# The inner layer norms' affine split between ScalarE and VectorE, rounded products first, and the last norm stored by half rows

## The chip, the cores and the metric

The kernel runs on one core of one Trainium2 chip. The metric is the time of one execution on the device in microseconds (us). The kernel before was timed three times: 1306.21, 1308.70 and 1308.98 us, median 1308.7. The profiled execution took 1311.17 us; its span, from the first to the last instruction of the trace, is 1309.4 us.

## What is computed

One sequence of 256 tokens of 1024 features goes through two blocks. The first has two layers (an attention and pooling mixer, then a gated linear attention mixer), each followed by an MLP; the second has a gated delta rule mixer with a spatial gating unit, and a mixture of 16 experts. Behind each mixer and each MLP stands a residual with a layer norm, six in all:

```python
def layer_norm(x, g, b):
    xf = x.astype(jnp.float32)
    mu = jnp.mean(xf, axis=-1, keepdims=True)
    var = jnp.mean(jnp.square(xf - mu), axis=-1, keepdims=True)
    return ((xf - mu) * lax.rsqrt(var + LN_EPS) * g + b).astype(x.dtype)
...
    x = layer_norm(ALPHA * x + mix, ln1_g[i], ln1_b[i])
    x = layer_norm(ALPHA * x + sqrelu_mlp(x, mlp_w1[i], mlp_w2[i]), ln2_g[i], ln2_b[i])
```

`mix` and the MLP end in a matmul over all features, and what follows a norm starts with one. So the norm stands between two stretches of TensorE work, and the weights of the first product behind it are on the chip before it begins.

## The kernel before

**Products.** Every weight matrix is streamed in chunks of 1 MB (128 partitions x 2048 numbers). SyncE loads a chunk into one of three slots of `ring`. ScalarE copies it, rounded to the matmul format, into `w_hi` (L1603); VectorE writes the rest, `ring - w_hi`, into `w_lo` (L1020). Activations are split in the same way (`x_hi`/`x_lo`, `o_hi`/`o_lo`). A product is three matmuls: hi*hi, hi*lo and lo*hi (`products`, L364 to L368). A chunk against 256 tokens is 48 matmuls of 256 columns (`by_feature`, `by_token`, `triples`), or 24 of 512 columns in the output projections (`by_rows`, `last_rows`). `take` (L358) waits until both parts of a chunk are there. `triples` is a generator that yields after every three matmuls, so that other products can be put in between.

**What sets the order.** Each engine's program is written out by hand in one block per engine. An engine works strictly in its own order and waits on semaphores: `full`/`evac` per PSUM bank, `hi_split` and `pieces_split` for weights, `normed`, `x_hi`, `x_split` for a norm. `split_ahead` puts the rounding of the next weights into the programs of ScalarE and VectorE just ahead of each read of a PSUM bank, as many chunks ahead as its argument says. SyncE issues the load of chunk n once VectorE has split chunk n-3.

**An inner norm** (five of the six, l = 0 to 4) works on two token halves t = 0, 1 of 128 tokens each, and on two feature halves.
- TensorE (`last_rows`, L450) ends the projection: token half 0 first, then the two halves of token half 1. Among the last of these it puts the eight transposes of token half 0 (`norm_transposes`, L509), then two triples of the next chunk (waiting on `x_split`), the eight transposes of token half 1, and the other 14 triples.
- VectorE (`moments`, L1040; `normalize`, L1053) adds the residual out of PSUM (L1047), takes the statistics (L1049, L1051) and writes `(x - mean) / deviation` to `res` (L1059). ScalarE takes the square root (L1625).
- The affine `* g + b` is applied to the transposed tile on its way out of PSUM into `n_v`. ScalarE does it for three of the four (token half, feature half) pairs, four tiles of 128 x 128 each (`high_half`, L1627, L1633), and rounds into `x_hi` (L1636). VectorE does the fourth (L1084, L1089). VectorE writes `x_lo` for all four (`low_half`, L1061, L1064).
- GpSimd computes the same affine for the token-major residual `xt` (`affine`, L2045: L2052 times g, L2053 plus b), while the MLP runs.

**The last norm** has no transposes: VectorE normalizes into `res`, GpSimd multiplies and adds over 1024 columns per token half, and SyncE stores each token half in one DMA (L2169).

## Time and profile before

| | |
|---|---|
| median of 3 runs | 1308.7 us |
| profiled execution, its span | 1311.17 us, 1309.4 us |
| PE (TensorE matmul) busy | 1265.4 us, 97% of the span |
| DVE (VectorE) busy | 832.6 us, 64% |
| ACT (ScalarE) busy | 600.5 us, 46% |
| POOL (GpSimd) busy | 170.2 us, 13% |
| mean granted TensorE clock | 0.987 |

Busy times of matmuls are modelled and overlap, so the share of PE says that it seldom stands still, not that it is at its peak. What a change near a norm is worth is read from the gaps between matmuls there: a timeline gives for each row its start, its duration and, in brackets, how long the engine stood idle before it and what ended that. Rows are merged where instructions of one line follow each other (x8); the start of the next row minus the start of this one is then what the group took.

### The profile page before, as it was taken

Reading aid. Unit: us, or ns where it says so; the run is one execution under the profiler, and the core shown is the slowest. Engines: PE = TensorE matmul, PEld = TensorE weight load, DVE = VectorE, ACT = ScalarE, POOL = GpSimd, SP = SyncE. Lnnn points to the kernel's source line nnn. Section 1 sums busy time; section 2 is a strip of 40 time slices with the busy share of each in tenths; the row PEclk is TensorE's granted clock in tenths of the full one; section 3 lists DMA queues with packets and bytes.
Section 4 is the critical chain, followed back from the end, with each engine's and each line's share of the span. In section 5 each row is a group of like instructions: output and inputs, shape, how many; then the busy total and the mean of one; then the engine's idle time right before and its main releaser. Section 6 shows DMA issues by size and latency. Waiting matters only on the chain.

```text
span 1309.4 us, 20713 instructions
## 1 busy us (share of the span) xinstructions
PE 1265.4 (97%) x8950; PEld 1180.4 (90%) x8950; DVE 832.6 (64%) x980; ACT 600.5 (46%) x697; POOL 170.2 (13%) x132
## 2 busy tenths in 40 slices
PE   7999999999999999999899999899999999999996
PEld 7977999998998899998889999899998999999995
DVE  6566865557655775556699448863776765555554
ACT  4464533335645533333575346624833543333331
POOL 8400400001300040000402200120000050000002
PEclk9999999999999999999989999999999999999999
DMA  9712575554643475558786447563764465555550
GB/s 269 172 65 97 165 238 182 189 192 122 201 161 97 132 255 181 181 187 142 129 143 101 97 91 126 110 107 55 225 206 162 139 204 180 187 192 191 180 176 33
DMA packets 160220, 205.02 MB, mean 157 GB/s; under 512 B 13571, under 2 KB 142322, under 8 KB 160130
## 3 DMA queue, kind: packets, MB, share of 16 engines
q1 hardware_dynamic: 157906, 195.80, 53.6%
q0 software_dynamic: 2224, 7.90, 2.0%
q8 instruction: 71, 1.16, 0.4%
q14 instruction: 19, 0.16, 0.0%
HBM read 202.63 MB, written 1.05 MB: 156 GB/s over the span
## 4 chain that ended last, share of the span: by engine, by line
PE 88%; DVE 5%; ACT 4%; DMA 2%; issue 1%; POOLq 0%; POOL 0%; DVEq 0%; ACTq 0%
PE PS L366 25%; PE PS L367 24%; PE PS L368 24%; DMA ring<-in_w_in 2%; DVE w_lo L1020 2%; PE PS L869 1%; PE PS L853 1%; PE PS L865 1%; PE PS L516 1%; ACT AR L1633 1%; ACT w_hi L1603 1%; PE PS L594 1%; PE PS L616 1%; PE PS L765 1%; PE PS L771 1%
## 5 line engine op out<-in xcount | busy, mean ns | idle before, releaser
L1020 DVE TENSOR_TENSOR w_lo<-ring,w_hi 128x2048 fp32r<-128x2048 f32 x182 | 434.7, 2392 | 207.1 <-ACT w_hi L1603 206.7
L366 PE MATMUL PS<-x_hi,w_hi 128*128 128x256 f32 x1648 | 477.2, 290 | 2.6 <-DVE w_lo L1115 2.1
L368 PE MATMUL PS<-x_hi,w_lo 128*128 128x256 f32 x1648 | 468.5, 284 | 0.0
L367 PE MATMUL PS<-x_lo,w_hi 128*128 128x256 f32 x1648 | 468.4, 284 | 0.0
L1603 ACT ACTIVATE w_hi<-ring 128x2048 fp32r<-128x2048 f32 x182 | 347.3, 1912 | 241.7 <-PE PS L368 229.2
L366 PEld LDWEIGHTS PS<-x_hi,w_hi 128*128 128x128 f32 x1648 | 318.6, 193 | 8.5 <-issue 3.4
L367 PEld LDWEIGHTS PS<-x_lo,w_hi 128*128 128x128 f32 x1648 | 318.4, 193 | 3.9 <-issue 2.2
L368 PEld LDWEIGHTS PS<-x_hi,w_lo 128*128 128x128 f32 x1648 | 318.0, 193 | 0.0
L1615 ACT ACTIVATE AR<-PS 128x512 f32<-128x512 f32 (+1 forms) x144 | 82.1, 586 | 306.5 <-PE PS L368 187.7
L366 PE MATMUL PS<-w_hi,o_hi 128*128 128x512 f32 x480 | 188.5, 393 | 1.3 <-ACT res L1615 0.8
L367 PE MATMUL PS<-w_lo,o_hi 128*128 128x512 f32 x480 | 187.4, 390 | 0.0
L368 PE MATMUL PS<-w_hi,o_lo 128*128 128x512 f32 x480 | 186.8, 389 | 0.0
L2052 POOL TENSOR_TENSOR xt<-res,gb 128x1024 f32<-128x1024 f32 x12 | 43.0, 3581 | 676.0 <-DVE res L1059 227.0
L366 PEld LDWEIGHTS PS<-w_hi,o_hi 128*128 128x128 f32 x480 | 90.3, 188 | 20.4 <-DVE o_lo L1234 1.5
L368 PEld LDWEIGHTS PS<-w_hi,o_lo 128*128 128x128 f32 x480 | 90.1, 188 | 19.2
L367 PEld LDWEIGHTS PS<-w_lo,o_hi 128*128 128x128 f32 x480 | 90.3, 188 | 16.6
L366 PE MATMUL PS<-w_hi,x_hi 128*128 128x256 f32 x256 | 77.1, 301 | 12.8 <-DVE x_lo L1064 12.0
L367 PE MATMUL PS<-w_lo,x_hi 128*128 128x256 f32 x256 | 74.3, 290 | 0.0
L368 PE MATMUL PS<-w_hi,x_lo 128*128 128x256 f32 x256 | 74.1, 289 | 0.0
L366 PEld LDWEIGHTS PS<-w_hi,x_hi 128*128 128x128 f32 x256 | 51.4, 201 | 15.2 <-issue 15.2
L1231 DVE TENSOR_TENSOR AR<-AR 128x512 f32<-128x512 f32 x32 | 23.2, 725 | 53.7 <-ACT AR L1615 53.7
L367 PEld LDWEIGHTS PS<-w_lo,x_hi 128*128 128x128 f32 x256 | 51.2, 200 | 0.2 <-issue 0.2
(370 smaller groups left out, 1341.4 us busy)
## 6 DMA issues: line engine op xcount, KB each, us to landing
ring<-in_mlp_w SPq DMA_DIRECT2D x64, 1024.0 KB, 5.3
ring<-in_w_in SPq DMA_DIRECT2D x32, 1024.0 KB, 11.5
ring<-in_expert_w_gate SPq DMA_DIRECT2D x16, 1024.0 KB, 5.4
ring<-in_expert_w_up SPq DMA_DIRECT2D x16, 1024.0 KB, 5.4
ring<-in_expert_w_down SPq DMA_DIRECT2D x16, 1024.0 KB, 4.9
ring<-in_c_w_in SPq DMA_DIRECT2D x12, 1024.0 KB, 5.5
ring<-in_a_w_in SPq DMA_DIRECT2D x4, 1024.0 KB, 8.6
ring<-in_c_w_out SPq DMA_DIRECT2D x4, 1024.0 KB, 5.0
```

The lines of the kernel that those rows point to most:

```text
L366: mm(out, a_hi, b_hi, start=first, stop=False, skip_group_check=True)
L367: mm(out, a_hi, b_lo, start=False, stop=False, skip_group_check=True)
L368: return mm(out, a_lo, b_hi, start=False, stop=last, skip_group_check=True)
L516: ins = nc.tensor.transpose(ps[:, i * P:(i + 1) * P], res[:, t, k * P:(k + 1) * P], ident[:])
L594: mm(ps[:, i * nk:(i + 1) * nk], a_q[:, head, t * P:(t + 1) * P], a_kk[:, g, a, 0:nk], start=True, stop=False, skip_group_check=True)
L616: ins = mm(PS[:, t, o:o + nh * P], a_v2[kb][:, a, 64 * g:64 * g + P], a_T[:, n % 3, kb * nh * P:(kb + 1) * nh * P], start=False, stop=(kb ...
L765: ins = mm(ps, ones[:], s_sq[:, j % 2].rearrange("p a b -> p (a b)"), start=True, stop=True)
L1020: v.tensor_tensor(w_lo[:, m % PARTS], ring[:, index[split[m]] % RING], w_hi[:, m % PARTS].bitcast(F32), ALU.subtract)\
L1231: after(v.tensor_tensor(h, h, h, ALU.mult))
L1603: a(w_hi[:, m % PARTS], ring[:, index[split[m]] % RING], ACT.Copy).then_inc(S("hi_split"), 1)
L1615: evacuated(a(out, ps if in_ is None else in_(ps), func, scale=scale), name)
L2052: after(gp.tensor_tensor(xt[:, t, :], res[:, t, :], gb[:, 0, :], ALU.mult))
```

## The change

1. **Rounded weight first.** `by_feature`, `by_token`, `triples` and `by_rows` now issue all products with `w_hi` first (32 of 48, or 16 of 24), waiting only for `hi_split`, and then those with `w_lo`, waiting for `pieces_split`. The number and shapes of matmuls stay. Not changed are the very first chunk (`halves`) and `last_rows`.
2. **Rounded x first in a norm.** The chunk behind an inner norm is taken by `with_norm`: 8 products with `x_hi` of a (token half, feature half) wait only for its `x_hi`; the 4 with `x_lo` come later. Twenty of them now stand ahead of the transposes of token half 1.
3. **Affine shared.** The four transposed tiles of a (token half, feature half) go to two banks of two tiles: ScalarE takes one bank, VectorE the other (`affine_half`). ScalarE then rounds all four into `x_hi`. VectorE loses its rounding (L1089) and gains the affine of 6 more tiles.
4. **Order on ScalarE.** In each inner norm the rounding of the next-but-one chunk moves ahead of token half 1's affine.
5. **Last norm.** VectorE does `(x - mean) * g` and `* 1/deviation + b` by halves of 512 columns with `scalar_tensor_tensor`; GpSimd is out of it. SyncE stores four half rows.

ScalarE in the first inner norm (`AR<-PS,vec` is the affine, `st<-st,cst` the square root), before:

```order
L1625 ACTIVATE st<-st,cst 128x1
L1633 ACTIVATE AR<-PS,vec 128x128 x4
L1636 ACTIVATE x_hi<-AR 128x4x128
L1633 ACTIVATE AR<-PS,vec 128x128 x4
L1636 ACTIVATE x_hi<-AR 128x4x128
L1625 ACTIVATE st<-st,cst 128x1
L1633 ACTIVATE AR<-PS,vec 128x128 x4
L1636 ACTIVATE x_hi<-AR 128x4x128
L1603 ACTIVATE w_hi<-ring 128x2048
```

and in the changed kernel:

```order
L1736 ACTIVATE st<-st,cst 128x1
L1744 ACTIVATE AR<-PS,vec 128x128 x2
L1748 ACTIVATE x_hi<-AR 128x4x128
L1744 ACTIVATE AR<-PS,vec 128x128 x2
L1748 ACTIVATE x_hi<-AR 128x4x128
L1736 ACTIVATE st<-st,cst 128x1
L1714 ACTIVATE w_hi<-ring 128x2048
L1744 ACTIVATE AR<-PS,vec 128x128 x2
L1748 ACTIVATE x_hi<-AR 128x4x128
L1744 ACTIVATE AR<-PS,vec 128x128 x2
L1748 ACTIVATE x_hi<-AR 128x4x128
```

Each affine group is halved, a fourth group is added, and the weight rounding stands ahead of token half 1.

VectorE from the reciprocal of token half 0 on, in the same norm, before:

```order
L1056 RECIPROCAL st<-st 128x1
L1059 TENSOR_SCALAR res<-res,st 128x512 x2
L1047 SCALAR_TENSOR_TENSOR res<-xt,PS 128x512
L1049 BN_STATS st<-res 128x6
L1047 SCALAR_TENSOR_TENSOR res<-xt,PS 128x512
L1049 BN_STATS st<-res 128x6
L1051 BN_AGGR st<-st 128x2
L1064 TENSOR_TENSOR x_lo<-AR,x_hi 128x4x128
L1056 RECIPROCAL st<-st 128x1
```

and in the changed kernel:

```order
L1139 RECIPROCAL st<-st 128x1
L1142 TENSOR_SCALAR res<-res,st 128x512 x2
L1128 SCALAR_TENSOR_TENSOR res<-xt,PS 128x512
L1130 BN_STATS st<-res 128x6
L1155 TENSOR_SCALAR AR<-PS,vec 128x128 x4
L1128 SCALAR_TENSOR_TENSOR res<-xt,PS 128x512
L1130 BN_STATS st<-res 128x6
L1134 BN_AGGR st<-st 128x2
L1148 TENSOR_TENSOR x_lo<-AR,x_hi 128x4x128
L1139 RECIPROCAL st<-st 128x1
```

Four affine tiles come in between the two column halves of token half 1.

VectorE at the end of the program (the last norm, from token half 1's first column half on), before:

```order
L1047 SCALAR_TENSOR_TENSOR res<-xt,PS 128x512
L1049 BN_STATS st<-res 128x6
L1047 SCALAR_TENSOR_TENSOR res<-xt,PS 128x512
L1049 BN_STATS st<-res 128x6
L1051 BN_AGGR st<-st 128x2
L1056 RECIPROCAL st<-st 128x1
L1059 TENSOR_SCALAR res<-res,st 128x512 x2
```

and in the changed kernel:

```order
L1128 SCALAR_TENSOR_TENSOR res<-xt,PS 128x512
L1130 BN_STATS st<-res 128x6
L1172 RECIPROCAL st<-st 128x1
L1175 SCALAR_TENSOR_TENSOR xt<-res,st,gb 128x512 x2
L1128 SCALAR_TENSOR_TENSOR res<-xt,PS 128x512
L1130 BN_STATS st<-res 128x6
L1134 BN_AGGR st<-st 128x2
L1168 SCALAR_TENSOR_TENSOR res<-res,st,gb 128x512 x2
L1172 RECIPROCAL st<-st 128x1
L1175 SCALAR_TENSOR_TENSOR xt<-res,st,gb 128x512 x2
```

The finish of token half 0 stands ahead of token half 1's last statistics, and what GpSimd did has come to VectorE.

The diff, cut to its core (`by_token`, `triples` and `by_rows` change as `by_feature` does):

```diff
+            def take_high(chunk):
+                m = part[chunk]
+                reached[0] = m + 1
+                pe.wait_ge(S("hi_split"), m + 1)
+                return m % PARTS
+            def take_low(chunk):
+                pe.wait_ge(S("pieces_split"), part[chunk] + 1)
+            def high_products(out, w, x, token, first):
+                for i in range(2):
+                    a, b = (x[i], w) if token else (w, x[i])
+                    mm(out, a, b, start=first and i == 0, stop=False, skip_group_check=True)
+            def low_product(out, w, x, token, last):
+                a, b = (x[0], w) if token else (w, x[0])
+                return mm(out, a, b, start=False, stop=last, skip_group_check=True)
...
-                        c = slice(m * P, (m + 1) * P)
-                        ins = products(ps[:, m * T:(m + 1) * T], wh[:, k, c], wl[:, k, c], a_hi[:, k, :], a_lo[:, k, :], k == 0, k == KT - 1)
+                        c, o = slice(m * P, (m + 1) * P), slice(m * T, (m + 1) * T)
+                        if halves is not None:
+                            ins = products(ps[:, o], wh[:, k, c], wl[:, k, c], a_hi[:, k, :], a_lo[:, k, :], k == 0, k == KT - 1)
+                        else:
+                            high_products(ps[:, o], wh[:, k, c], (a_hi[:, k, :], a_lo[:, k, :]), False, (m, k) == (0, 0))
+                if halves is None:
+                    take_low(chunk)
+                    for m in range(2):
+                        for k in range(KT):
+                            c, o = slice(m * P, (m + 1) * P), slice(m * T, (m + 1) * T)
+                            ins = low_product(ps[:, o], wl[:, k, c], (a_hi[:, k, :],), False, k == KT - 1)
                 close(ins, chunk, chunk)
...
+            def with_norm(chunk, bank, l):
                 n = take(chunk)
                 wh, wl = colview(w_hi, n), colview(w_lo, n)
                 ps = claim(pe, chunk, bank)
-                for m in range(2):
-                    for k in range(KT):
-                        if k % 4 == 0 and layer is not None:
-                            pe.wait_ge(S("x_split"), 4 * (layer + 1) + 2 * m + k // 4 + 1)
-                        c, o = slice(m * P, (m + 1) * P), slice(m * T, (m + 1) * T)
-                        if token:
-                            ins = products(ps[:, o], x_hi[:, k, c], x_lo[:, k, c], wh[:, k, :], wl[:, k, :], k == 0, k == KT - 1)
-                        else:
-                            ins = products(ps[:, o], wh[:, k, c], wl[:, k, c], x_hi[:, k, :], x_lo[:, k, :], k == 0, k == KT - 1)
-                        if (m, k) == (1, KT - 1):
-                            close(ins, chunk, chunk)
-                            filled.append(chunk)
-                        yield
+                def high(m, b):
+                    pe.wait_ge(S("x_hi"), 4 * l + 2 * m + b + 1)
+                    for k in range(4 * b, 4 * b + 4):
+                        for i, w in enumerate((wh, wl)):
+                            mm(ps[:, m * T:(m + 1) * T], x_hi[:, k, m * P:(m + 1) * P], w[:, k, :],
+                               start=(m, k, i) == (0, 0, 0), stop=False, skip_group_check=True)
+                def low(m, b):
+                    pe.wait_ge(S("x_split"), 4 * (l + 1) + 2 * m + b + 1)
+                    for k in range(4 * b, 4 * b + 4):
+                        ins = mm(ps[:, m * T:(m + 1) * T], x_lo[:, k, m * P:(m + 1) * P], wh[:, k, :],
+                                 start=False, stop=k == KT - 1, skip_group_check=True)
+                    return ins
+                high(0, 0)
+                high(0, 1)
+                low(0, 0)
+                yield
+                low(0, 1)
+                high(1, 0)
+                low(1, 0)
+                high(1, 1)
+                close(low(1, 1), chunk, chunk)
+                filled.append(chunk)
...
-                    steps = triples(then, 0, True, ln)
-                    advance(steps, 2)
+                    steps = with_norm(then, 0, ln)
+                    advance(steps, 1)
                     norm_transposes(ln, 1)
                     return steps
...
             def norm_transposes(l, t):
                 for b in range(2):
-                    ps = claim(pe, (f"nT{l}", t, b), 4 + 2 * t + b)
                     pe.wait_ge(S("normed"), 2 * (TT * l + t) + b + 1)
-                    for i in range(4):
-                        k = 4 * b + i
-                        ins = nc.tensor.transpose(ps[:, i * P:(i + 1) * P], res[:, t, k * P:(k + 1) * P], ident[:])
-                    close(ins, (f"nT{l}", t, b))
+                    for e in range(2):
+                        ps = claim(pe, (f"nT{l}", t, b, e), 4 + 2 * b + e)
+                        for i in range(2):
+                            k = 4 * b + 2 * e + i
+                            ins = nc.tensor.transpose(ps[:, i * P:(i + 1) * P], res[:, t, k * P:(k + 1) * P], ident[:])
+                        close(ins, (f"nT{l}", t, b, e))
...
-            def moments(l, t, alpha):
+            def moments(l, t, alpha, halves=(0, 1)):
-                for n in range(2):
+                for n in halves:
...
+                if n == 0:
+                    return
...
+                ve.wait_ge(S("x_hi"), 4 * l + 2 * t + b + 1)
                 ks, ts = slice(4 * b, 4 * b + 4), slice(t * P, (t + 1) * P)
                 v.tensor_tensor(x_lo[:, ks, ts], n_v[:, ks, ts], x_hi[:, ks, ts].bitcast(F32), ALU.subtract).then_inc(S("x_split"), 1)
-            def layer_norm(l, alpha, last=False):
+            def affine_half(l, t, b):
+                ps = bank((f"nT{l}", t, b, 1), 0 if t else 1)
+                for i in range(2):
+                    k = 4 * b + 2 + i
+                    ins = v.tensor_scalar(n_v[:, k, t * P:(t + 1) * P], ps[:, i * P:(i + 1) * P], col(f"g{l}", k), col(f"b{l}", k), ALU.mult, ALU.add)
+                evacuated(ins, (f"nT{l}", t, b, 1))
+            def last_norm(l, alpha):
+                ve.wait_ge(S("affine"), 32 * 7)
+                def half(ap, t, n):
+                    return ap[:, t, n * BANK:(n + 1) * BANK]
+                def centred(t):
+                    ve.wait_ge(S("variance"), n_norm[0] * TT + t + 1)
+                    for n in range(2):
+                        r = half(res, t, n)
+                        v.scalar_tensor_tensor(r, r, st[:, 16 * t + 12:16 * t + 13], half(gb, 0, n), ALU.subtract, ALU.mult).then_inc(S("centred"), 1)
+                def scaled(t):
+                    ve.wait_ge(S("deviation"), n_norm[0] * TT + t + 1)
+                    after(v.reciprocal(st[:, 16 * t + 15:16 * t + 16], st[:, 16 * t + 14:16 * t + 15]))
+                    for n in range(2):
+                        ve.wait_ge(S("centred"), 2 * t + n + 1)
+                        v.scalar_tensor_tensor(half(xt, t, n), half(res, t, n), st[:, 16 * t + 15:16 * t + 16], half(gb, 1, n), ALU.mult, ALU.add)\
+                            .then_inc(S("xt_ready"), 1)
+                moments(l, 0, alpha)
+                centred(0)
+                moments(l, 1, alpha, (0,))
+                scaled(0)
+                moments(l, 1, alpha, (1,))
+                centred(1)
+                scaled(1)
+            def layer_norm(l, alpha):
                 moments(l, 0, alpha)
                 normalize(0)
-                moments(l, 1, alpha)
-                if not last:
-                    ve.wait_ge(S("x_hi"), 3 * l + 1)
-                    low_half(l, 0, 0)
+                moments(l, 1, alpha, (0,))
+                affine_half(l, 0, 0)
+                affine_half(l, 0, 1)
+                moments(l, 1, alpha, (1,))
+                low_half(l, 0, 0)
                 normalize(1)
                 n_norm[0] += 1
-                if last:
-                    return
-                ve.wait_ge(S("x_hi"), 3 * l + 2)
                 low_half(l, 0, 1)
-                ts = slice(P, 2 * P)
-                ps = bank((f"nT{l}", 1, 1), 0)
-                for i in range(4):
-                    k = 4 + i
-                    ins = v.tensor_scalar(n_v[:, k, ts], ps[:, i * P:(i + 1) * P], col(f"g{l}", k), col(f"b{l}", k), ALU.mult, ALU.add)
-                evacuated(ins, (f"nT{l}", 1, 1))
-                ve.wait_ge(S("x_hi"), 3 * l + 3)
+                affine_half(l, 1, 0)
+                affine_half(l, 1, 1)
                 low_half(l, 1, 0)
-                read((f"nT{l}", 1, 1), 0)
-                after(v.tensor_copy(x_hi[:, 4:8, ts], n_v[:, 4:8, ts]))
                 low_half(l, 1, 1)
...
             def high_half(l, t, b):
-                ps = bank((f"nT{l}", t, b), 0 if t else 1)
+                ps = bank((f"nT{l}", t, b, 0), 0 if t else 1)
                 ks, ts = slice(4 * b, 4 * b + 4), slice(t * P, (t + 1) * P)
-                for i in range(4):
+                for i in range(2):
                     k = 4 * b + i
                     ins = a(n_v[:, k, ts], ps[:, i * P:(i + 1) * P], ACT.Identity, scale=col(f"g{l}", k), bias=col(f"b{l}", k))
-                evacuated(ins, (f"nT{l}", t, b))
-                read_out(act, (f"nT{l}", t, b))
+                evacuated(ins, (f"nT{l}", t, b, 0))
+                for e in range(2):
+                    read_out(act, (f"nT{l}", t, b, e))
                 a(x_hi[:, ks, ts], n_v[:, ks, ts], ACT.Copy).then_inc(S("x_hi"), 1)
             def layer_norm(l, last=False):
...
                 deviation(1)
                 n_norm[0] += 1
                 if not last:
+                    split_ahead(pieces_for[(f"nT{l}", 1, 0, 0)], 1)
                     high_half(l, 1, 0)
+                    high_half(l, 1, 1)
...
-            affine(6, 5)
...
-            for t in range(TT):
-                sp.wait_ge(S("xt_ready"), 5 * TT + t + 1)
-                sp.dma_start(out[0, t * P:(t + 1) * P, :], xt[:, t, :]).then_inc(S("stored"), 16)
-            sp.wait_ge(S("stored"), 16 * TT)
+            for i in range(2 * TT):
+                t, c = i // 2, slice(i % 2 * BANK, (i % 2 + 1) * BANK)
+                sp.wait_ge(S("xt_ready"), 5 * TT + i + 1)
+                sp.dma_start(out[0, t * P:(t + 1) * P, c], xt[:, t, c]).then_inc(S("stored"), 16)
```

## Rows read from the trace of the kernel before

**Rows 1.** The page (busy, share), and TensorE's waits: total us, times, longest.
```profile
PE 1265.4 (97%) x8950; PEld 1180.4 (90%) x8950; DVE 832.6 (64%) x980; ACT 600.5 (46%) x697; POOL 170.2 (13%) x132
...
PE PS L366 <- DVE x_lo L1064: 12.0, 5, 2.4
...
PE PS L366 <- DVE w_lo L1020: 0.3, 1, 0.3
```

**Rows 2.** Timeline of TensorE, first inner norm: start, us, what [idle before].
```profile
123.06 1.03 PE L516 MATMUL PS<-ident,res 128*128 128x128 f32 x8
123.85 0.48 PE L366 MATMUL PS<-w_hi,o_hi 128*128 128x512 f32 x1
...
125.09 0.40 PE L368 MATMUL PS<-w_hi,o_lo 128*128 128x512 f32 x1
127.89 0.36 PE L366 MATMUL PS<-w_hi,x_hi 128*128 128x256 f32 x1 [2.40 <-DVE x_lo L1064]
...
129.02 1.94 PE L516 MATMUL PS<-ident,res 128*128 128x128 f32 x8 [0.18 <-DVE res L1059]
...
136.41 0.28 PE L368 MATMUL PS<-w_hi,x_lo 128*128 128x256 f32 x1
136.53 0.36 PE L366 MATMUL PS<-x_hi,w_hi 128*128 128x256 f32 x1
```

**Rows 3.** Timeline of VectorE in the same norm.
```profile
123.12 0.69 DVE L1049 BATCH_NORM_STATS2 st<-res 128x6 f32<-128x512 f32 x1
125.52 0.69 DVE L1047 SCALAR_TENSOR_TENSOR res<-xt,PS 128x512 f32<-128x512 f32 x1 [1.71 <-PE PS L368]
...
126.97 0.21 DVE L1051 BATCH_NORM_AGGREGATE st<-st 128x2 f32<-128x12 f32 x1
127.10 0.64 DVE L1064 TENSOR_TENSOR x_lo<-AR,x_hi 128x512 fp32r<-128x512 f32 x1
...
128.33 1.00 DVE L1059 TENSOR_SCALAR res<-res,st 128x512 f32<-128x512 f32 x2
...
131.00 1.37 DVE L1084 TENSOR_SCALAR AR<-PS,vec 128x128 f32<-128x128 f32 x4 [1.07 <-PE PS L516]
...
134.15 2.29 DVE L1020 TENSOR_TENSOR w_lo<-ring,w_hi 128x2048 fp32r<-128x2048 f32 x1
```

**Rows 4.** Timeline of ScalarE in the same norm.
```profile
123.69 1.50 ACT L1633 ACTIVATE AR<-PS,vec 128x128 f32<-128x128 f32 x4 [2.44 <-PE PS L516]
125.23 0.63 ACT L1636 ACTIVATE x_hi<-AR 128x512 fp32r<-128x512 f32 x1
...
127.82 0.28 ACT L1625 ACTIVATE st<-st,cst 128x1 f32<-128x1 f32 x1
...
132.22 1.90 ACT L1603 ACTIVATE w_hi<-ring 128x2048 fp32r<-128x2048 f32 x1
```

**Rows 5.** Stretches: PE, PEld, DVE, ACT, POOL busy; granted clock; DMA share; GB/s.
```profile
64.00:80.00 16.00, 13.61 (x103) 11.42 (x103) 10.25 (x19) 9.26 (x40) 0.00 (x0) 1.00 0.30 98
...
130.60:131.20 0.60, 0.60 (x5) 0.60 (x4) 0.20 (x1) 0.60 (x4) 0.00 (x0) 0.50 0.00 0
```

**Rows 6.** Waits of ScalarE for weights of the second block.
```profile
ACT w_hi L1603 <- DMA ring<-in_w_in: 7.1, 4, 5.1
```

**Rows 7.** Timelines of VectorE and GpSimd at the end.
```profile
1297.92 0.69 DVE L1047 SCALAR_TENSOR_TENSOR res<-xt,PS 128x512 f32<-128x512 f32 x1 [0.86 <-PE PS L368]
...
1300.14 1.28 DVE L1059 TENSOR_SCALAR res<-res,st 128x512 f32<-128x512 f32 x2
...
1303.99 2.34 POOL L2053 TENSOR_TENSOR xt<-xt,gb 128x1024 f32<-128x1024 f32 x1
```

**Rows 8.** DMA issues at the end: count, KB each, us to landing.
```profile
out_x<-xt SPq DMA_DIRECT2D x2, 512.0 KB, 2.6
```

**Rows 9.** VectorE, a three-operand instruction with all operands in SBUF.
```profile
777.29 1.41 DVE L1322 SCALAR_TENSOR_TENSOR AR<-AR,vec,res 128x512 f32<-128x512 f32 x2
```

More of the change, by code:

```diff
@@ L375, in by_feature @@
                 else:
-                    n = take(chunk)
+                    n = take_high(chunk)
                 wh, wl = colview(w_hi, n), colview(w_lo, n)
@@ L420, in by_token @@
             def by_token(chunk, lo=0, hi=8):
-                n = take(chunk)
+                n = take_high(chunk)
                 wh, wl = colview(w_hi, n), colview(w_lo, n)
```

54 lines of the change are left out of this document (44 added, 10 removed).

## Prediction

> **What bounds the kernel now.** I read the page first, then the waits of TensorE, then the timelines of three engines in the first inner norm, then the end of the program. TensorE is busy for 97% of the span, and its longest total wait is on one line, the writing of `x_lo` in VectorE, five times, 12.0 us together; the wait for an ordinary `w_lo` comes once and is 0.3 us [rows 1]. So the bound is TensorE's own work, and a gain can come only from its gaps: the five inner norms, and the end, where TensorE has finished.
>
> The inner norm, from the first transpose at 123.06 to the first matmul of the next chunk but one at 136.53, takes 13.47 us [rows 2]. Its work is less. Eight transposes take 0.79 (123.06 to 123.85). The six matmuls of 512 columns behind them end their issue at 125.09 + 0.23 = 125.32, so 1.47. The chunk is 48 matmuls at a pitch of 0.12 (136.41 to 136.53), 5.76, and the second eight transposes are another 0.79. Together 8.81; 4.66 us are lost. Of that, 2.57 (125.32 to 127.89) is the wait for the first `x_lo`. The rest lies around the second transposes and in a slower clock: in the stretch after the wait the granted clock is 0.50, that is 1.2 instead of 2.4 GHz, while matmuls are waiting to go [rows 5]. All five norms show the same wait (12.0 / 5 = 2.4) [rows 1].
>
> **Inner norms, step by step** (first norm; 0.05 to 0.1 us per hand-over between engines, as between rows 3 and 2).
> - *First x_hi.* ScalarE's four affine tiles take 1.50, so 0.375 each; VectorE's four take 1.37, so 0.34 each [rows 3, 4]. Two tiles need only the first two transposes, two pitches of 0.1 earlier: ScalarE runs from 123.49 to 124.24. VectorE is free at 123.12 + 0.69 = 123.81 and has its two done at 124.53. The rounding (0.63) then ends at 125.20 instead of 125.86. TensorE reaches the chunk at 125.32 and does 8 products (0.96) without waiting, to 126.28.
> - *Second x_hi.* The same again on ScalarE: affine to 125.85, rounding to 126.5. TensorE waits 0.25 and has the next 8 done at 127.5. VectorE's other two tiles end at about 125.2, before the last bank of the projection is full at 125.52, so that step is not pushed back [rows 3].
> - *First x_lo.* It stands behind that bank's residual and statistics and ends at 127.10 + 0.64 = 127.74 as before. The four products follow at 127.85 to 128.33. What was a gap of 2.57 is now about 0.6 in two pieces.
> - *Normalizing token half 1.* The square root came at 127.82, since ScalarE was still rounding; now ScalarE is free, and it comes at about 127.2 [rows 4]. Normalizing then starts right behind `x_lo`, at 127.95 and not 128.33: the second transposes start 0.38 earlier, at 128.64, and end at 129.55.
> - *Token half 1.* The moved weight rounding occupies ScalarE from 127.5 to 129.4 (1.90) [rows 4]. Its tiles could start at 128.95, so the move costs about 0.45 here. Affine to 130.2 on both engines, rounding to 130.9; TensorE, done with the four products of the second `x_lo` at 130.13, waits about 0.85, the largest gap left. Then 8 + 4 + 8 + 4 products: 131.0 to 131.96, 132.44, 133.4 and 133.9. The second rounding ends at 132.2 and the last `x_lo` at 132.85, both in time.
> - *What is late next.* The chunk ends at 133.9 instead of 136.53. Before, the next chunk's `w_lo` was ready at 134.15 + 2.29 = 136.44, just in time [rows 3]. Now it follows the last `x_lo` at 132.85 and ends at 135.15. With the old order of products TensorE would wait 1.25 for it; with the rounded weight first it asks for `w_lo` only 32 x 0.12 = 3.84 into the chunk, at 137.7. Its `w_hi` has been there since 129.4. This is the whole use of the new order: elsewhere it can save 0.3 at most [rows 1].
>
> Gain per norm 136.53 - 133.9 = 2.6, five norms 13.1. Bounds: below, 1.3 per norm, if the clock falls as before (first rival); above, 3.3, if the weight rounding is hidden and the hand-overs are shorter. Nothing in the trace splits a product in this order; I take the middle, as the durations are those of the same instructions.
>
> **Products elsewhere.** The same matmuls at the same pitch: 0. One place loses: where a chunk follows its operand pair by pair (the first after the gating unit), 4 products of 0.12 per pair now stand before the next wait instead of 6, against 0.69 of VectorE work per pair. Three times up to 0.2: I take 0.4 lost. GpSimd, SyncE's queue for weights and the ring slots keep their order.
>
> **The end.** TensorE's last result is taken at 1297.92. From there the chain is residual, statistics, square root, normalizing (from 1300.14), GpSimd times g and plus b until 1303.99 + 2.34 = 1306.33, and the store, landing in 2.6, at 1309.0 [rows 7, 8]. Now VectorE first finishes token half 0: `(x-mean)*g` costs 0.70 per 512 columns by the row of an instruction with three operands in SBUF (1.41 for two) [rows 9], against 0.5 for normalizing. That puts the residual of the last bank at about 1298.5, 0.6 late. Statistics and their aggregate end at 1300.2, the first pass at 1301.55, the reciprocal at 1301.75, the two last halves at 1302.4 and 1303.1. The store of the last half starts at 1303.1 and moves 256 KB, half of the 2.6 us store. Its landing is not shown: 1.3 if it went by size alone, 2.6 if size did not matter; I take 2.2, so 1305.3. Gain 1309.0 - 1305.3 = 3.7, between 3.3 and 4.6.
>
> The Trainium skill (DMA: Bandwidth & Descriptors) puts a fixed cost of about 2.0 us on each DMA, most of it completion, which speaks against cutting a store into halves. By that rule the last half would land in about 2.3 and the gain would be 3.6; the trace's 2.6 us for 512 KB agrees with a large fixed part.
>
> **Sum.** 13.1 - 0.4 + 3.7 = 16.4. The profiled execution took 1311.2, which is 2.5 above the median of 1308.7; I take the same difference from the median: 1292.3.
>
> **Rivals.**
> 1. *The clock falls all the same.* The granted clock was 0.50 after each gap of 2.57 us. In another stretch with a gap between matmul groups and 2.4 us of idle time in 16 it stayed at 1.00 [rows 5]. The new norm has some 2 us of gaps in 8.6, none over 0.9, which is nearer to the second. For it: the gaps lie close together. If the clock is halved from about 129 to 132.4 as before, the 2.3 us of matmuls there take 4.6, of which about 1 us fills gaps: 1.3 lost per norm, 6.5 in all, 1298.8. The Trainium skill (TensorE: Matmul & The Clock Gate, Part 1) says that the clock follows how busy TensorE has recently been, which leaves this open; no row shows the new pattern.
> 2. *A later wait takes the gain.* The mixer of the second block loads chunks slower than it uses them at times: ScalarE waits for them four times, 7.1 us in all [rows 6]. If the load behind the fourth norm does not keep up with the earlier start, its 2.6 are lost: 1295. If ScalarE's moved weight rounding has to wait for a load or a slot in every norm, all of token half 1 waits behind it, as do its affine tiles and the next PSUM copies; one more us each gives 1297.5, two give 1302.5. Against it: the loads of the next chunk are issued well before the norm begins.
> 3. *Slower: the new order raises the pitch.* Some 6000 matmuls are issued in another order; accumulating the same columns of a bank is now split into two passes, and `by_rows` changes bank eight times instead of four. If the pitch of 0.12 grew by more than 16.4 us / 6000 = 2.7 ns, or 2%, everything would be lost; 5 ns more each gives 1322. Against it: the stationary operand is loaded anew for every matmul already (8950 loads for 8950 matmuls [rows 1]).
> 4. *It does not do what it says:* if TensorE still waits for the first `x_lo` (VectorE's affine tiles late), only the end gains: 1305.
>
> **How the numbers follow.** Forecast 0.60; clock 0.19; later waits 0.12; no effect in the norms 0.04; slower 0.05. The forecast's own range is 1289 to 1295.5 by the bounds of the norms and the store. The first two rivals reach to 1299 and beyond; the range 1288.5 to 1299.5 leaves out about 0.15 to 0.2. A difference of 0.2% (2.6 us) is about what can be told from none here. Slower by more: 0.04; within it: 0.03, the rest faster.
>
> **What the profile will show.** TensorE's wait for `x_lo` falls from 12.0 to under 3 us; a gap of about 0.8 before the first product of token half 1, on ScalarE's `x_hi`; no wait for the next chunk's `w_lo`; granted clock 1.00 through the norm and its mean near 0.99; the pitch of 0.12 unchanged in the MLP; DVE rows of about 0.7 at the end and no GpSimd; 7.5 us from TensorE's last result to the landing instead of 11.1. Wrong would be a pitch above 0.122, a clock of 0.50 in the norms, or a new wait over 1 us on ScalarE's weight rounding.

## The result and the profile after

The changed kernel took 1295.3 us (median of 4; 1294.59 to 1297.95) against 1308.7 (4 runs) of the kernel before: ratio 0.9901, interval 0.9885 to 0.9916, so 13.0 us faster (11.0 to 15.0). Two later comparisons of the same kernel gave 0.9885 (0.9867 to 0.9904) and 0.9903 (0.9889 to 0.9917). The mean of the three, 0.9896, is 13.6 us. Forecast were 1292.3 and a gain of 16.4; the time lies in the range.

The page after (busy) and TensorE's longest waits, which answer to [rows 1]:

```profile
PE 1260.1 (97%) x8950; PEld 1171.7 (90%) x8950; DVE 841.1 (65%) x999; ACT 597.1 (46%) x682; POOL 160.5 (12%) x128
...
PE PS L846 <- ACT AR L1944: 6.7, 2, 4.7
...
PE PS L454 <- ACT x_hi L1748: 4.3, 7, 0.9
PE PS L877 <- DVE s_sc L1421: 3.2, 1, 3.2
```

The 12.0 us on `x_lo` are gone; 4.3 on `x_hi` are left, none over 0.9. VectorE has 19 instructions more: in each of five norms four more affine tiles (eight instead of four, not the six more that the section on the change gives it) and one rounding less, and four in the last norm. L846 and L877 are in the mixer of the second block (the squared norms of q and k, and the gates of the delta rule); what they mean comes below.

The first inner norm on TensorE, as [rows 2]:

```profile
122.47 1.04 PE L597 MATMUL PS<-ident,res 128*128 128x128 f32 x8
...
124.85 0.36 PE L454 MATMUL PS<-w_hi,x_hi 128*128 128x256 f32 x1
...
127.86 1.11 PE L597 MATMUL PS<-ident,res 128*128 128x128 f32 x8
128.91 0.74 PE L460 MATMUL PS<-w_hi,x_lo 128*128 128x256 f32 x4
130.28 0.38 PE L454 MATMUL PS<-w_hi,x_hi 128*128 128x256 f32 x1 [0.63 <-ACT x_hi L1748]
...
133.25 0.28 PE L435 MATMUL PS<-x_hi,w_hi 128*128 128x256 f32 x1
```

From 122.47 to 133.25 it takes 10.78 us instead of 13.47. The granted clock there, one row for the last 4.3 us (columns as [rows 5]):

```profile
128.91:133.25 4.34, 3.71 (x29) 3.51 (x29) 3.55 (x7) 2.46 (x6) 0.00 (x0) 1.00 0.00 0
```

VectorE and then ScalarE in the same norm, as [rows 3, 4]:

```profile
128.77 1.36 DVE L1155 TENSOR_SCALAR AR<-PS,vec 128x128 f32<-128x128 f32 x4
...
132.23 2.28 DVE L1101 TENSOR_TENSOR w_lo<-ring,w_hi 128x2048 fp32r<-128x2048 f32 x1
```

```profile
126.82 1.90 ACT L1714 ACTIVATE w_hi<-ring 128x2048 fp32r<-128x2048 f32 x1
128.63 0.78 ACT L1744 ACTIVATE AR<-PS,vec 128x128 f32<-128x128 f32 x2
129.59 0.63 ACT L1748 ACTIVATE x_hi<-AR 128x512 fp32r<-128x512 f32 x1 [0.18 <-DVE AR L1155]
```

`w_lo` ends at 132.23 + 2.28 = 134.51, which is 1.26 after the chunk that needs it has begun, and TensorE does not wait for it.

The end of the program, VectorE and the stores, as [rows 7, 8]:

```profile
1282.48 0.69 DVE L1130 BATCH_NORM_STATS2 st<-res 128x6 f32<-128x512 f32 x1
...
1292.29 1.42 DVE L1175 SCALAR_TENSOR_TENSOR xt<-res,st,gb 128x512 f32<-128x512 f32 x2
```

```profile
out_x<-xt SPq DMA_DIRECT2D x4, 256.0 KB, 2.1
```

From the first statistics of the last norm to the end of the span: 1296.2 - 1282.48 = 13.72 us. Before, those statistics began at 1291.92 and the span ended at 1309.4, so 17.48: 3.76 less.

**Where the lead grows.** The start of each norm's first statistics on VectorE, in us, for the kernel before, and how much earlier it comes in three executions of the changed kernel:

| norm | before | after | again | again_2 |
|---|---|---|---|---|
| first | 118.67 | 0.60 | 0.68 | -1.22 |
| second | 306.12 | 3.28 | 3.38 | 1.49 |
| third | 429.81 | 5.85 | 5.96 | 4.08 |
| fourth | 617.80 | 8.03 | 8.45 | 6.56 |
| fifth | 1006.19 | 6.83 | 10.02 | 9.12 |
| last | 1291.92 | 9.44 | 12.63 | 11.72 |

From one line to the next the first two norms give 2.7 and 2.6, and the third, with the mixer behind it, 2.2 to 2.5. By the first rows of ScalarE behind the fourth and fifth norms, these give 2.3 and 2.6. What differs is the start (1.9 us between executions of one kernel) and the stretch between the fourth norm and the fifth, the mixer of the second block.

### The profile page after: what moved, and what is told of

Read it like the earlier page. It is cut to its first block, busy times and chain, and to the rows that moved or that the text cites. A ratio compares the mean times of both kernels' runs of the same rounds, so it can differ in the third digit from the quotient of the medians.

```text
span 1296.2 us, 20746 instructions
## 1 busy us (share of the span) xinstructions
PE 1260.1 (97%) x8950; PEld 1171.7 (90%) x8950; DVE 841.1 (65%) x999; ACT 597.1 (46%) x682; POOL 160.5 (12%) x128
## 3 DMA queue, kind: packets, MB, share of 16 engines
q8 instruction: 71, 1.16, 0.4%
## 4 chain that ended last, share of the span: by engine, by line
PE 81%; DVE 9%; DMA 4%; ACT 4%; issue 2%; DVEq 0%; ACTq 0%
PE PS L379 37%; PE PS L384 18%; PE PS L435 8%; DMA ring<-in_w_in 4%; DVE w_lo L1101 3%; ACT w_hi L1714 1%; PE PS L950 1%; PE PS L934 1%; PE PS L388 1%; PE PS L390 1%; PE PS L389 1%; PE PS L946 1%; DVE AR L1477 1%; DVE st L1130 1%; DVE res L1128 1%
## 5 line engine op out<-in xcount | busy, mean ns | idle before, releaser
L379 PE MATMUL PS<-x_hi,w_hi 128*128 128x256 f32 x1312 | 319.8, 284 | 0.2 <-DVE x_lo L1611 0.2
L379 PE MATMUL PS<-x_lo,w_hi 128*128 128x256 f32 x1312 | 318.4, 283 | 0.0
L384 PE MATMUL PS<-x_hi,w_lo 128*128 128x256 f32 x1312 | 170.8, 283 | 0.0
L384 PEld LDWEIGHTS PS<-x_hi,w_lo 128*128 128x128 f32 x1312 | 163.3, 192 | 0.0
L379 PE MATMUL PS<-w_hi,o_hi 128*128 128x512 f32 x384 | 150.3, 391 | 1.6 <-DVE o_lo L1345 0.8
L379 PE MATMUL PS<-w_hi,o_lo 128*128 128x512 f32 x384 | 150.0, 391 | 0.0
L384 PE MATMUL PS<-w_lo,o_hi 128*128 128x512 f32 x384 | 94.8, 389 | 0.0
L379 PEld LDWEIGHTS PS<-w_hi,o_hi 128*128 128x128 f32 x384 | 72.3, 188 | 16.1 <-DVE o_lo L1345 1.2
L384 PEld LDWEIGHTS PS<-w_lo,o_hi 128*128 128x128 f32 x384 | 72.1, 188 | 15.0
L435 PE MATMUL PS<-x_hi,w_hi 128*128 128x256 f32 x320 | 85.5, 302 | 0.0
L379 PEld LDWEIGHTS PS<-w_hi,o_lo 128*128 128x128 f32 x384 | 72.3, 188 | 13.9
L435 PE MATMUL PS<-x_lo,w_hi 128*128 128x256 f32 x320 | 80.9, 287 | 0.0
L435 PE MATMUL PS<-x_hi,w_lo 128*128 128x256 f32 x320 | 45.4, 287 | 0.0
```

Source lines behind the costliest of these rows:

```text
L379: mm(out, a, b, start=first and i == 0, stop=False, skip_group_check=True)
L384: return mm(out, a, b, start=False, stop=last, skip_group_check=True)
L435: ins = mm(ps[:, o], a, b, start=(low, m, k, i) == (0, 0, 0, 0), stop=bool(low) and k == KT - 1, skip_group_check=True)
```

## Experiments

A ratio is to the kernel before, run beside it on the same chip.

**The changed kernel again** (`again`).

> The changed kernel once more, unchanged, as the measure for the runs beside it. Theory: what is missing from the predicted gain (13.3 us measured, 16.4 predicted) is lost in the second block's mixer by waits that belong to the kernel and come back in every execution. Then the ratio is 0.990 again, and between the fourth and the fifth norm the trace again loses 3 to 4 us of the lead over the kernel before: ScalarE's weight rounding waits twice for loads there, 4.5 and 3.0 us, TensorE's wait on the squared norms of q and k (the matmul of norm_sums) totals 6 to 7 us, and the w_lo beside GpSimd's affine takes 3.3 us instead of 2.3. Rival: the load times differ from one execution to the next; then the second wait on a load is nearer the 1.0 us of before and the profiled time about 1295.

Measured: 1294.4, ratio 0.9885. Half the theory held. The wait for the gates was 3.2 again and `w_lo` 3.31, but the lead grew from 8.45 at the fourth norm to 10.3 at the spatial gating unit, where in the first execution it fell from 8.03 to 7.11. The second load wait was 2.4 us, against 3.0. So most of what the first trace lost between the fourth and the fifth norm was not the kernel's, but that of one execution. The old norms show such a loss too: TensorE's wait on the squared norms, 4.5 us in the trace of before and 6.7, 6.0 and 5.0 in the three of the changed kernel, is 6.4 in `tail_only`, the next experiment, where no norm ahead of it was changed.

**The last norm alone** (`tail_only`: the kernel before with `last_norm` and four half-row stores).

```diff
-            layer_norm(5, ALPHA2, last=True)
+            last_norm(5, ALPHA2)
...
-            affine(6, 5)
```

> The kernel before with only the last norm changed: VectorE does it by halves of 512 columns, and SyncE stores four half rows. Theory: the end is independent of the rest, so the gain is the 3.8 us that the two traces show there (18.21 against 14.44 from the first statistics of the last norm to the end), 1308.7 - 3.8 = 1304.9, ratio 0.9971. Rival: part of the 3.8 is work that TensorE finished earlier in the changed kernel; then the gain is 2 to 3 us, 1306 or so.

Measured: 1304.7, ratio 0.9963 (0.9950 to 0.9976), 4.8 us faster (3.1 to 6.5). In its trace the end takes 1306.1 - 1292.43 = 13.67, as in the changed kernel:

```profile
1292.43 0.69 DVE L1049 BATCH_NORM_STATS2 st<-res 128x6 f32<-128x512 f32 x1
```

The theory holds: the end gains the same with the old inner norms as with the new.

**The order of products alone** (`order_only`: the kernel before with `take_high`/`take_low` in four loops).

> The kernel before with only the rounded-weight-first order in by_feature, by_token, triples and by_rows; the chunk with a norm, the affine split and the end as before. Theory: 0 to -0.6 us, as TensorE waited only 0.3 us for an ordinary w_lo in all, and the first product behind the gating unit loses 0.3; 1308 to 1309, ratio 0.9995 to 1.0005. Rival A: the new order raises the pitch of matmuls; 1 ns each on 6000 matmuls is 6 us, ratio 1.005. Rival B: the order helps by itself in the attention parts, where w_lo takes 4.5 us beside GpSimd; then -2 us or more.

Measured: 1309.1, ratio 0.9997 (0.9985 to 1.0008). No gain, and no rise of the pitch that the time could show: rival A's 6 us are excluded, and rival B's 2 us lie at the very edge of the interval.

**The new order without its use** (`wait_both`).

```diff
             def take_high(chunk):
...
-                pe.wait_ge(S("hi_split"), m + 1)
+                pe.wait_ge(S("pieces_split"), m + 1)
```

> The changed kernel, in which the products with the rounded weight wait for both parts of the weight at the start of the chunk; the order of products stays. Theory: in each inner norm the next chunk's w_lo ends 1.2 us after the chunk could begin (first norm: 132.23 + 2.28 = 134.5 against 133.25), so each norm loses 1.25, five norms 6.3, and with other chunks some more: 1301 to 1302, ratio to the kernel before 0.9950. Rival: the lead of the norms is mostly given back later anyway, or VectorE is ahead; then less than 2 us is lost, 1297.

Measured: 1298.0, ratio 0.9915 (0.9899 to 0.9931), 3.9 us slower than the changed kernel beside it, and 2.5 by the mean of its three ratios. TensorE's waits in its trace, behind the first, second and fourth norms (behind the third it is 1.16):

```profile
136.33 0.38 PE L435 MATMUL PS<-x_hi,w_hi 128*128 128x256 f32 x1 [1.15 <-DVE w_lo L1101]
...
322.08 0.39 PE L379 MATMUL PS<-x_hi,w_hi 128*128 128x256 f32 x1 [1.67 <-DVE w_lo L1101]
...
630.57 0.38 PE L379 MATMUL PS<-x_hi,w_hi 128*128 128x256 f32 x1 [1.17 <-DVE w_lo L1101]
```

Together 5.15, four times and not five: behind the fifth norm, where the router's products stand, TensorE has no such wait. The order is worth nothing that shows by itself; once the norms are short it hides these 5.15 us, of which the times show 2.5 to 3.9. 1.0 comes back at the gates: after the wait behind the fourth norm GpSimd's multiplication is over before VectorE's `w_lo` begins, `w_lo` takes 2.27 and not 3.31, and the wait for the gates is 2.2, not 3.2.

```profile
637.15 2.38 POOL L2166 TENSOR_TENSOR xt<-res,gb 128x1024 f32<-128x1024 f32 x1
```

```profile
639.79 2.27 DVE L1101 TENSOR_TENSOR w_lo<-ring,w_hi 128x2048 fp32r<-128x2048 f32 x1
```

**ScalarE does all of the affine** (`no_share`).

```diff
-                affine_half(l, 0, 0)
-                affine_half(l, 0, 1)
...
-                ps = bank((f"nT{l}", t, b, 0), 0 if t else 1)
...
-                for i in range(2):
+                for e in range(2):
+                    ps = bank((f"nT{l}", t, b, e), 0 if t else 1)
```

> The changed kernel, in which ScalarE alone does the affine of all transposed tiles of an inner norm; the order of products, with those of the rounded x first, and all else stay. Theory: a round of ScalarE (affine, then rounding) takes 1.50 + 0.63 = 2.1 us instead of 1.4, so in a norm the first x_hi comes 0.7 later and the second 1.4 later, and the same in token half 1: each norm ends its chunk about 1.4 later, five norms 7; 1302, ratio 0.9940. Rival: VectorE, relieved of 2 x 1.37 us per norm, does its residual, statistics and x_lo earlier, and TensorE loses only the first 0.7: 3.5 us in all, ratio 0.9915.

Measured: 1304.0, ratio 0.9956 (0.9938 to 0.9973), some 7.9 us slower than the changed kernel by the mean ratio of 0.9896. The first gap of its first norm, and the longest:

```profile
124.86 0.36 PE L454 MATMUL PS<-w_hi,x_hi 128*128 128x256 f32 x1 [0.38 <-ACT x_hi L1745]
...
131.13 0.39 PE L454 MATMUL PS<-w_hi,x_hi 128*128 128x256 f32 x1 [1.20 <-ACT x_hi L1745]
```

There are four such gaps in each norm (20 waits, 14.2 us in all), one for each round of ScalarE. The theory holds and the rival falls, though a norm loses more than the 1.4 us expected: the first takes 134.79 - 122.07 = 12.72, 1.9 more than in the changed kernel.

**Triples again in the norm** (`norm_triples`).

```diff
-                high(0, 0)
-                high(0, 1)
-                low(0, 0)
...
+                        if k % 4 == 0:
+                            pe.wait_ge(S("x_split"), 4 * (l + 1) + 2 * m + k // 4 + 1)
...
+                        ins = products(ps[:, o], x_hi[:, k, c], x_lo[:, k, c], wh[:, k, :], wl[:, k, :], k == 0, k == KT - 1)
```

> The changed kernel, in which the chunk behind an inner norm is again taken in triples (both products of the rounded x and the one of x_lo together, after x_lo), six matmuls ahead of the second transposes; the shared affine, the split banks and all else stay. Theory: TensorE again waits for the first x_lo, which VectorE ends at 126.50 + 0.64 = 127.1 in the first norm, so the gap is 2.4 us, the clock falls to the lower level behind it as in the kernel before, and each norm loses 1.5 to 2.2 of its 2.7; about 9 us, 1303 to 1304, ratio 0.9955. Rival: the gap alone is lost and caught up by the slack before token half 1, 0.6 per norm, 3 in all, ratio 0.991.

Measured: 1302.6, ratio 0.9945 (0.9926 to 0.9964), 6.4 us slower by the same mean; between the two theories, and the trace says why. TensorE in the first norm, then in the fourth, then in the fifth:

```profile
129.01 0.36 PE L388 MATMUL PS<-w_hi,x_hi 128*128 128x256 f32 x1 [2.40 <-DVE x_lo L1134]
129.21 0.28 PE L389 MATMUL PS<-w_lo,x_hi 128*128 128x256 f32 x1
129.33 0.28 PE L390 MATMUL PS<-w_hi,x_lo 128*128 128x256 f32 x1
...
622.23 0.36 PE L388 MATMUL PS<-w_hi,x_hi 128*128 128x256 f32 x1 [2.90 <-DVE x_lo L1134]
...
1009.03 0.55 PE L388 MATMUL PS<-w_hi,x_hi 128*128 128x256 f32 x1 [2.47 <-DVE x_lo L1134]
1009.38 0.41 PE L389 MATMUL PS<-w_lo,x_hi 128*128 128x256 f32 x1
1009.59 0.41 PE L390 MATMUL PS<-w_hi,x_lo 128*128 128x256 f32 x1
```

Nearly the same gap is followed by a pitch of 0.12 in the first norm and 0.21 in the fifth. In the fourth the granted clock is 0.50 from 623.1 to 626.5. The first three norms, with the clock at 1.00, lost about 0.7 each against the changed kernel, the fourth 2.3 and the fifth 2.2, some 6.6 together; so the clock costs some 1.5 us in a norm in which it falls. In the first norm there is no clock loss, and it still takes 135.70 - 124.21 = 11.49: of the 2.69 that the change saves, 2.0 come with the shared affine and a clock that stays up, 0.7 with the order of products. How much of the 2.0 is the clock's can be estimated from the two old norms in which it stayed at 1.00: the fifth of `tail_only` took 12.55 us and the third of `before_gap` 13.00, where both take 13.45 in the kernel before; so 0.4 to 0.9.

**The weight rounding not moved** (`no_moved`).

```diff
-                    split_ahead(pieces_for[(f"nT{l}", 1, 0, 0)], 1)
```

> The changed kernel without the fourth point of the change: in each inner norm ScalarE rounds the next-but-one chunk behind token half 1's affine again, not ahead of it. Theory, as the prediction put it: the moved rounding holds up token half 1 by 0.45 us per norm, so without it the gap before x_hi of token half 1 (0.63 to 0.8) shrinks and each norm is 0.45 shorter: -2.2 us, 1292, ratio 0.9865. Rival: the weight rounding then ends at about 132.9 in the first norm, w_lo and w_hi of the next chunks come late and TensorE waits there; 0 to +3 us. A third outcome: the gap is set by the square root and the normalizing on VectorE, not by ScalarE; then nothing changes.

Measured: 1297.6, ratio 0.9912 (0.9895 to 0.9930), 2.1 us slower by the mean, which is not clear of noise: the interval takes in the mean of 0.9896. The 2.2 us faster that were expected are excluded. ScalarE in its first norm:

```profile
128.23 0.81 ACT L1744 ACTIVATE AR<-PS,vec 128x128 f32<-128x128 f32 x2 [1.41 <-PE PS L597]
129.49 0.63 ACT L1748 ACTIVATE x_hi<-AR 128x512 fp32r<-128x512 f32 x1 [0.46 <-DVE AR L1155]
```

The affine does start 0.40 earlier, but the rounding then waits 0.46 for VectorE's tiles: 129.49 against 129.59, which is how much earlier this whole execution runs. So the moved rounding costs nothing. Without it ScalarE rounds two chunks in a row behind the second norm (315.94 to 319.64), `w_lo` follows late, and TensorE waits for it in the middle of a chunk:

```profile
322.70 2.17 PE L384 MATMUL PS<-x_hi,w_lo 128*128 128x256 f32 x16 [0.72 <-DVE w_lo L1101]
```

From the second norm to the third the lead over the kernel before grows by 1.3 us here (3.36 to 4.67) and by 2.6 in each trace of the changed kernel.

**GpSimd held back** (`gp_late`).

```diff
+            pool.wait_ge(S("dn_gates"), 1)
             affine(3, 3)
```

> The changed kernel, in which GpSimd's affine for xt behind the fourth norm waits until the gates of the gated delta rule are done, so that it no longer runs beside VectorE's w_lo at the start of that mixer. Theory: this w_lo took 3.3 us instead of 2.3 beside GpSimd in both executions of the changed kernel, in the chain to the scalars that TensorE waits for (3.2 us instead of 2.2); without it the wait is 2.2 again and the kernel 1.0 us faster, below what the time can show, but seen in the trace as a lead of 10.3 us over the kernel before that is not cut to 9.3 in the first 10 us behind the fourth norm. Rival: the slowed w_lo has another cause (its own reads and ScalarE's); then the wait stays 3.2. Against both: GpSimd's affine now meets other VectorE work later.

Measured: 1301.1, ratio 0.9932 (0.9918 to 0.9946), slower by 4.7. The wait for the gates fell not by 1.0 but by 3.0, to 0.21:

```profile
641.28 0.61 PE L877 MATMUL PS<-s_sc,tri 128*128 128x8 f32 x4 [0.21 <-DVE s_sc L1421]
```

Then GpSimd's four operations met VectorE's next two `w_lo`, and TensorE waited 9.2 us at L846. VectorE in this kernel, and the first of GpSimd's operations beside it:

```profile
633.13 2.27 DVE L1101 TENSOR_TENSOR w_lo<-ring,w_hi 128x2048 fp32r<-128x2048 f32 x1
...
635.53 0.17 DVE L1415 TENSOR_TENSOR s_sc<-s_ab,adt 128x16 f32<-128x16 f32 x1
...
644.67 8.87 DVE L1101 TENSOR_TENSOR w_lo<-ring,w_hi 128x2048 fp32r<-128x2048 f32 x2
```

```profile
641.31 2.88 POOL L2166 TENSOR_TENSOR xt<-res,gb 128x1024 f32<-128x1024 f32 x1 [176.16 <-DVE s_sc L1421]
```

**GpSimd's last addition in VectorE's pause** (`gp_gap`, and `before_gap` for the kernel before), with the changed kernel once more beside them (`again_2`).

```diff
+                    if (l, t) == (3, 1):
+                        pool.wait_ge(S("ab_ready"), 1)
                     gp.tensor_tensor(xt[:, t, :], xt[:, t, :], gb[:, 1, :], ALU.add).then_inc(S("xt_ready"), 1)
```

> The changed kernel once more, beside the next two on the same chip. The two comparisons so far gave ratios of 0.990 and 0.9885; expected 0.989. In the trace: each inner norm gives 2.3 to 2.7 us over the kernel before, 12.6 in all, and behind the fourth norm the waits for the gates of the gated delta rule are 3.2 us again, as w_lo takes 3.3 us and the 16-element addition behind it 2.16 us beside GpSimd. The stretch from the fourth to the fifth norm differs from one execution to the next (303.5 and 300.7 us so far) by its loads; a third value is to be had.

> The changed kernel, in which only GpSimd's last addition behind the fourth norm (plus b of token half 1) waits until VectorE has done the small addition that leads to the gates (ab_ready); it then falls into the 4.95 us in which VectorE waits for ScalarE. Theory: w_lo takes 2.3 us again instead of 3.3 and the small addition 0.17 instead of 2.16, TensorE's wait for the gates falls from 3.2 us to 0.2, nothing is delayed in its place, and the kernel is 3.0 us faster than the changed one: ratio 0.9865 to the kernel before. Rival: as when all of GpSimd's affine was held back there, VectorE's later w_lo are slowed instead (4.4 us instead of 2.25 each) and a wait of several us comes on the squared norms of q and k; then the same or slower than the changed kernel.

> The kernel before with that same wait of GpSimd's last addition behind the fourth norm. Theory: the kernel before lost 2.2 us there of the 3.2 (its w_lo took 2.27 already, its small addition 2.16), so it gains 2.0, ratio 0.9985; and between it and the changed kernel with the same wait the difference is 1.0 larger than between the two kernels themselves, which is the part that the earlier start of the change lost to GpSimd. Rival: the loss of the change there has another cause, and both gain the same 2 to 3 us.

Measured: `again_2` 1295.7, ratio 0.9903 (0.9889 to 0.9917); `gp_gap` 1294.3, 0.9887 (0.9871 to 0.9904); `before_gap` 1310.0, 1.0012 (1.0000 to 1.0023). VectorE in `gp_gap`:

```profile
634.98 3.33 DVE L1101 TENSOR_TENSOR w_lo<-ring,w_hi 128x2048 fp32r<-128x2048 f32 x1
...
638.45 0.18 DVE L1415 TENSOR_TENSOR s_sc<-s_ab,adt 128x16 f32<-128x16 f32 x1
```

GpSimd beside it:

```profile
633.77 2.39 POOL L2166 TENSOR_TENSOR xt<-res,gb 128x1024 f32<-128x1024 f32 x1
638.77 2.40 POOL L2169 TENSOR_TENSOR xt<-xt,gb 128x1024 f32<-128x1024 f32 x1 [2.61 <-DVE s_sc L1415]
```

The small addition is short again (0.18; 2.16 in the changed kernel and before), so it was GpSimd's addition that held it. `w_lo` stays at 3.33: GpSimd's multiplication ends at 633.77 + 2.39 = 636.16. With its undisturbed 2.28 from there `w_lo` would end at 638.4, and it ends at 638.3. It is not slowed but waits its turn. The wait for the gates fell from 3.2 to 1.3, and the waits behind it in the same trace are:

```profile
PE PS L846 <- ACT AR L1944: 5.7, 2, 3.5
...
PE PS L846 <- ACT AR L1935: 2.3, 1, 2.3
```

The second is new: 2.3 us come back. `before_gap` has the like (2.5), though its wait for the gates fell from 2.2 to 0.2 as expected. The traces show where the gain goes. ScalarE's first row behind the small addition comes 2.12 us earlier in `gp_gap` than in `again_2` (638.65 against 640.77), but then the next chunk of that mixer has not landed, and ScalarE waits for it:

```profile
646.93 1.91 ACT L1714 ACTIVATE w_hi<-ring 128x2048 fp32r<-128x2048 f32 x1 [1.59 <-DMA ring<-in_w_in]
...
651.51 0.22 ACT L1972 ACTIVATE s_sc<-s_sc 128x16 f32<-128x16 f32 x1 [2.67 <-DVE s_sc L1451]
```

and in `again_2`, which rounds that chunk without waiting:

```profile
652.33 0.22 ACT L1972 ACTIVATE s_sc<-s_sc 128x16 f32<-128x16 f32 x1 [2.94 <-DVE s_sc L1451]
```

Of the 2.12 us, 0.82 are left. `before_gap` waits 1.77 us at the same chunk, before not at all. So a load takes back most of this gain; no run moved that load, so this is read from four traces and not tested. `gp_gap` has the lowest median of the three runs made side by side, but its interval covers the changed kernel's ratios: no version is shown to beat the change. Whether the edit gains anything stays open; the ratios that were expected, 0.9865 and 0.9985, lie outside both intervals, the first one just outside.

## Why the prediction was right, and where it was not

*Inner norms, 13.1.* Right. The first norm was forecast at 133.9 - 123.06 = 10.84 and took 10.78; the five give 2.7, 2.6, 2.4, 2.3 and 2.6, 12.6 together. The parts `no_share`, `norm_triples` and `wait_both` lose 7.9, 6.4 and 3.9 us, more than 12.6 in sum: they are not terms of a sum. The order of products is the clear case: it gains nothing alone and is needed once the norms are short.

*The first rival, the clock.* It did not fall in any of the five norms. But `norm_triples` shows that it need not have fallen after a gap of 2.4 us either. The prediction read the fall as belonging to the gap, as the one trace it had showed it five times of five; it is one outcome of two: a norm in triples costs 0.7 more, or 2.2 to 2.3. The loss of 1.3 per norm that the rival put on it was near the 1.5 seen there. Gaps up to 1.67 us (`no_share`, `wait_both`) showed no such loss in any norm.

*The moved rounding costs 0.45 here.* Wrong. The step took ScalarE for the bound of the first `x_hi` of token half 1; VectorE's two tiles, behind an `x_lo`, end later [`no_moved`]. The forecast gap of 0.85 came as 0.89 us (128.91 + 4 x 0.12 to 130.28), so the number survived the wrong reason. What the move is for was missed: the rounding of the chunk after next, 1.3 us behind the second norm by the trace, 2.1 in all by the medians, which is not clear of noise.

*w_lo later.* Right: TensorE does not wait, and would wait 1.15 to 1.67 behind four norms (`wait_both`); elsewhere the order gains nothing that shows (`order_only`).

*Pair by pair behind the gating unit, -0.4.* The lead fell there by 0.28 in every trace of the changed kernel. Right in sign and size.

*The end, 3.7.* 3.76, with a landing of 2.1 where 2.2 was taken.

*Later waits, the second rival.* In part, and not by its mechanism. The loads did not take the gain of the change behind the fourth norm, though they took most of the further 2 us in `gp_gap`. GpSimd took 1.0 of it. Before, its second multiplication ended just ahead of the `w_lo` in the chain to the gates; the norm brought `w_lo` forward by 10.3 us and GpSimd by 8.9, so that they now overlap by 1.2:

```profile
641.32 2.39 POOL L2052 TENSOR_TENSOR xt<-res,gb 128x1024 f32<-128x1024 f32 x1
```

```profile
643.99 2.27 DVE L1020 TENSOR_TENSOR w_lo<-ring,w_hi 128x2048 fp32r<-128x2048 f32 x1
```

```profile
632.45 2.39 POOL L2166 TENSOR_TENSOR xt<-res,gb 128x1024 f32<-128x1024 f32 x1
```

```profile
633.68 3.31 DVE L1101 TENSOR_TENSOR w_lo<-ring,w_hi 128x2048 fp32r<-128x2048 f32 x1
```

(The first two are of the kernel before, the last two of the changed one.) So the wait for the gates is 3.2 instead of 2.2, in all three executions, and 2.2 again in `wait_both`, where the two don't overlap. No term of the sum had GpSimd in it: this one was put at nothing.

*Slower, and no effect.* The third and fourth rivals did not come: `order_only` shows no cost of the order, and no wait for `x_lo` of a norm is left.

The terms as measured: 12.6 - 0.3 + 3.8 - 1.0 = 15.1, against 16.4 forecast and 13.6 by the comparisons, whose intervals reach 15.0, 17.4 and 14.5. The forecast was 1.3 too high by its terms; the rest, 1.5, is not assigned. One candidate, not tested, is that the old norms were read from a trace in which the clock fell in all five, and in `tail_only` and `before_gap` it fell in four of five. The 1295.3 us measured lie at the upper end of the 1289 to 1295.5 that the forecast gave for itself without a rival.

## What to carry to other kernels

When a gap is closed on the bounding engine, ask what else was timed to that gap: here the next chunk's `w_lo` became late by 1.2 to 1.7 us, and the reordered products that gain nothing alone were needed to hide it. Where two engines share a step, the rounding or reduction behind it starts with the slower one; a delay on the other is free up to the difference. And before explaining a few missing us from two traces, take the same kernel's trace again: here the same stretch of 310 us differed by 3.7 us between executions.

## What was not expected of the hardware

**The clock behind a gap of about 2 us is not fixed.** In the mixer of the second block TensorE waits at the same place in three executions of the same program; first of the changed kernel, then `again`, then `again_2`:

```profile
676.13 2.76 PE L846 MATMUL PS<-AR,ones 128*128 128x512 f32 x4 [2.06 <-ACT AR L1944]
```

```profile
675.52 1.96 PE L846 MATMUL PS<-AR,ones 128*128 128x512 f32 x4 [1.88 <-ACT AR L1944]
```

```profile
677.40 3.44 PE L846 MATMUL PS<-AR,ones 128*128 128x512 f32 x4 [1.95 <-ACT AR L1944]
```

Four matmuls of 512 columns took 1.96 us with the granted clock at 1.00 (2.4 GHz) throughout. It fell to 0.50 (1.2 GHz) at 677.1 in the first of the three, 1.0 after they began, and at 677.7 in the last, 0.3 after: 2.76 and 3.44. In the norms, gaps of 2.40 us and more (up to 2.90) were followed by the lower clock in 18 of 20 norms of the old form (before, `order_only`, `tail_only`, `before_gap`) and in 2 of 5 in `norm_triples`. What decides between the outcomes no run here shows.

The start differs in the same way. In the changed kernel the clock is 1.00 as the first chunk's products begin (10.4 us), falls to 0.50 between 11.3 and 12.1, and is back at 1.00 from 15.0 in the first execution, 14.7 in `again` and 19.0 in `again_2`; the first norm begins 1.9 us later in the last than in `again`.

**GpSimd and VectorE take turns.** Where both work from SBUF with two operands, one instruction waits for the whole of the other: a `w_lo` of 2.28 us took 3.33 as it began 1.2 behind a multiplication of 2.39, two in a row took 8.87 instead of 4.6 (`gp_late`), GpSimd's own operation 4.3 instead of 2.4, and a VectorE addition of 16 numbers per partition 2.16 instead of 0.17. The Trainium skill (SBUF: State Buffer, Who interferes with whom) has it so: the two share a pair of ports, held for the whole instruction, and a VectorE operation with two inputs in SBUF takes part in it. The traces agree: by that rule `w_lo` would end at 638.4 in `gp_gap`, and it ends at 638.3. How much is lost then depends on who begins first, and an edit that moves one of the two by 1 us can change it: in `norm_triples`, where `w_lo` comes later behind the norm, it takes 3.78 and the small addition 0.17.
